# Seven half-size products in place of eight for the convolution and gate projections of a hybrid decoder layer

## What is computed

```python
proj = jnp.einsum('bld,de->ble', rmsnorm(h, norm_mix), w_in)
rq, rk, rv, rg, dqkv, dz, da, db, gate_a, gate_b = jnp.split(proj, ...)
# branch A: retention, per-head RMS norm, swish gate
o_r = rms_plain(retention(q, k, v, ...)) * jax.nn.silu(rg)
# branch B: causal convolution of width 4 and Silu over 1536 channels
xpad = jnp.concatenate([s_conv, dqkv], axis=1)
conv = xpad[:, 0:L] * conv_w[0]
for j in range(1, 4):
    conv = conv + xpad[:, j:j + L] * conv_w[j]
cq, ck, cv = split(silu(conv))          # 512 channels each
g = -exp(a_log) * softplus(da + dt_bias); beta = sigmoid(db)
o_d = gated_delta(l2norm(cq), l2norm(ck), cv, g, beta)   # a triangular solve per chunk
o_d = rms_plain(o_d) * dn_norm * silu(dz)
```

## Time and profile before

| | |
|---|---|
| median of 3 timed runs | 820.1 us (819.86 to 820.67) |
| the profiled execution | 820.44 us, span of its instructions 818.6 us |
| TensorE matmuls | 798.8 us busy, 98% of the span |
| VectorE / ScalarE / GpSimd | 403.5 / 221.5 / 154.3 us busy |
| TensorE's granted clock | 0.998 of full speed on the mean |

### The profile page before, as it was taken

One profiled execution on the slowest core, in us unless ns is written; L12 is line 12 of the kernel. 1 busy time (PEld: TensorE's weight loads), 2 busy tenths in 40 slices (PEclk: granted clock), 3 DMA queues, 4 the chain that ended last, 5 costly groups with the idle time before them and its releaser, 6 DMA issues. The chain is left out here.

```text
span 818.6 us, 12786 instructions
## 1 busy us (share of the span) xinstructions
PE 798.8 (98%) x5138; PEld 500.9 (61%) x5138; DVE 403.5 (49%) x848; ACT 221.5 (27%) x483; POOL 154.3 (19%) x182
## 2 busy tenths in 40 slices
PE   9999999999999999999999999999899999999995
PEld 4446777778879887777777776455333333334443
DVE  4223555677647424664853458726342101105976
ACT  3202152595224311131001110122121111115275
POOL 0324420041054314200220043000100001004100
PEclk9999999999999999999999999999999999999999
DMA  9620354613020200523252024035899999995211
GB/s 361 228 87 22 116 181 155 170 64 111 1 104 3 104 2 13 206 94 82 102 205 78 26 103 151 34 132 210 317 395 357 426 421 423 402 394 193 75 52 64
DMA packets 21303, 136.40 MB, mean 167 GB/s; under 512 B 2492, under 2 KB 3276, under 8 KB 13948
## 3 DMA queue, kind: packets, MB, share of 16 engines
q1 hardware_dynamic: 13328, 103.08, 32.6%
q0 software_dynamic: 4720, 23.83, 8.0%
q10 hardware_dynamic: 3196, 8.66, 3.6%
HBM read 120.12 MB, written 19.64 MB: 171 GB/s over the span
## 5 line engine op out<-in xcount | busy, mean ns | idle before, releaser
L818 PE MATMUL pair<-mem 128*128 128x288 f32 x640 | 158.4, 407 | 0.0
L818 PEld LDWEIGHTS pair<-mem 128*128 128x128 f32 x640 | 120.5, 190 | 35.7 <-ACT mem L1505 1.6
L987 PE MATMUL single<-mem 128*128 128x288 f32 x448 | 110.0, 407 | 0.3
L987 PEld LDWEIGHTS single<-mem 128*128 128x128 f32 x448 | 84.7, 190 | 25.7 <-issue 1.6
L1372 PE MATMUL single<-mem 128*32 128x512 f32 x768 | 85.1, 594 | 0.9 <-DVE mem L2543 0.9
L1505 ACT ACTIVATE mem<-single 128x256 f32<-128x256 f32 (+6 forms) x104 | 41.9, 413 | 126.8 <-PE single L1233 48.5
L1505 ACT ACTIVATE mem<-pair 128x512 f32<-128x512 f32 (+5 forms) x83 | 36.6, 488 | 143.3 <-PE pair L1320 46.8
L2536 DVE SCALAR_TENSOR_TENSOR mem<-single,mem 128x256 f32<-128x256 f32 x12 | 5.8, 485 | 102.3 <-PE single L1372 91.1
L1372 PEld LDWEIGHTS single<-mem 128*32 128x32 f32 x768 | 23.6, 110 | 52.8 <-issue 51.7
L1224 PE MATMUL pair<-mem 128*128 128x512 f32 x112 | 51.0, 601 | 0.0
L1441 PE MATMUL pair<-mem 128*128 128x512 f32 x112 | 49.4, 595 | 0.3 <-DVE mem L2604 0.3
(11 more groups left out here) (435 smaller groups left out, 1126.3 us busy)
## 6 DMA issues: line engine op xcount, KB each, us to landing
mem<-in_w_gu SPq DMA_DIRECT2D x17, 2048.0 KB, 13.6
mem<-in_w_down SPq DMA_DIRECT2D x17, 1024.0 KB, 13.4
y_slots<-mem SPq DMA_DIRECT2D x9, 512.0 KB, 9.5
y_slots<-in_zeros POOLq DMA_DIRECT2D x8, 512.0 KB, 8.7
mem<-in_w_ga SPq DMA_DIRECT2D x2, 2048.0 KB, 9.1
mem<-in_w_gb SPq DMA_DIRECT2D x2, 2048.0 KB, 8.2
mem<-in_w_wo SPq DMA_DIRECT2D x2, 2048.0 KB, 8.1
mem<-in_w_pg SPq DMA_DIRECT2D x2, 2048.0 KB, 17.1
```

Of the source, the lines that this page charges most:

```text
L818: last = nc.tensor.matmul(pb[:, hf, 0:HALF], w(k), rhs[:, k, hf * HALF:(hf + 1) * HALF], start=(k == 0), stop=(k == kk - 1))
L987: last = nc.tensor.matmul(single[plan.buf[s]][:, 0:HALF], lhs[:, k, :], rhs[:, k, :], start=(k == 0 and j in (0, 1, 3, 4)), stop=(k == 3), ...
```

## The change

All twenty blocks are computed in ten groups of two blocks, group 0 to 5 for the convolution, 6 and 7 for `rg`, 8 and 9 for `dz`. A group is seven products p1, p2, p5, p6, p3, p7, p4 of four matmuls each, 128x288, that add up in PSUM banks. ScalarE empties p1, p5, p6 and p4 (step `fa`), VectorE adds p2, p3 and p7 to what was kept (step `fd`). Four products need sums of weights. They are made by the step `fS`, four additions of 128x512 for a group, all on GpSimd. The token sums (`uS`, before `wT`) are made at the start of the stage and lie where the third place of the ring was, so the ring has two places until the last chunk.

The convolution's first tap goes to ScalarE with the small copies (step `ct`), taps 2 to 4 stay on VectorE and run over 600 columns. Silu runs over four blocks at once (128x2304), three times in all. The squares for `rN` go from GpSimd to ScalarE, `rN` is copied from PSUM first and the square root becomes a step of its own (`nS`). The small DMAs of the decay rows (`g_rows`) and the norm rows (`n_rows`) move from ScalarE's queue to SyncE's, behind the weight chunks.

```diff
@@ schedule()
-    for m in range(2, NCONV):
-        s += [("cv", m), ("cvt", m), ("cvs", m - 1)] + ([("rOt",)] if m == 2 else []) + between[m]
...
+    low = lambda g: [("cvt", 2 * g)] + sums(g + 1)
+    high = lambda g: [("ct", 2 * g + 1), ("cvt", 2 * g + 1)]
+    sums = lambda g: [("fS", g, 0), ("fS", g, 1)]
+    def middle(g, p2=(), p5=(), p6=(), p3=()):
+        return ([f(g, "p2")] + list(p2) + [f(g, "p5")] + list(p5) + [f(g, "p6")] + list(p6) + [f(g, "p3")]
+                + ([("ct", 2 * g)] if g < NCG else []) + list(p3) + [f(g, "p7")])
+    s += [("uS", 0), ("uS", 1), ("ab",), ("uS", 2), ("uS", 3), f(0, "p1"), ("abT",)]
+    s += middle(0, p6=[("abF",)]) + low(0) + ...
+    s += low(1) + [f(2, "p1"), f(1, "p4")] + high(1)
+    s += middle(2, p6=[("cvs", 0)]) + [("rN",), f(2, "p4"), ("gE", 0)] + low(2)
+    s += [f(3, "p1")] + high(2) + middle(3, p6=[("nS",), ("nr", "rN")], p3=[("gE", 1), ("gE", 2)]) + low(3)
+    s += [f(4, "p1"), f(3, "p4")] + high(3) + middle(4, p6=[("cvs", 1)], p3=[("gE", 3)] + nf[0:2]) + low(4)
+    s += [f(5, "p1"), ("gs", 0), f(4, "p4"), ("gs", 1)] + high(4)
...
@@ TensorE
-                elif k0 in ("cv", "rg", "dz"):
-                    gemm_channels(s, lambda k: w[:, k, m * P:(m + 1) * P], uT, KD)
+                elif k0 in ("fa", "fd"):
+                    lhs = {"p1": w[0][0], "p2": w[0][1], "p5": wfast[0], "p6": wfast[1], "p3": wfast[2], "p7": w[1][0], "p4": w[1][1]}[name]
+                    rhs = {"p1": fast_rows(0, 0), "p2": fast_rows(1, 0), "p5": usum[0], "p6": usum[1], "p3": fast_rows(1, 1),
+                           "p7": fast_rows(0, 1), "p4": usum[2]}[name]
+                    if name in ("p5", "p6", "p3", "p7"):
+                        pe.wait_ge(sem("fsum"), 4 * g + {"p5": 1, "p6": 2, "p3": 3, "p7": 4}[name])
+                    for k in range(4):
+                        last = nc.tensor.matmul(group_bank(s), lhs[:, k, :], rhs[:, k, :], ...)
@@ ScalarE
+                elif k0 == "ct":
+                    copy(smp[:, :, 0:3], cst[:, m, :, :])
+                    copy(cnew[:, m, 0:3], cbuf[m % 4][:, 512:515])
+                    link(copy(cnew[:, m, 3:27].rearrange("p (b l) -> p b l", b=NB), smp[:, :, 8:11]))
+                    copy(acc[m % 2][:, 0:600], cbuf[m % 4][:, 0:600], conv_w[:, m, 0:1]).then_inc(sem("cnew"), 1)
@@ GpSimd
+                elif k0 == "fS" and s[1] in POOL_SUMS:
+                    if i == 0:
+                        pool.wait_ge(sem(f"ring{place(n)}"), landed(n))
+                        if g:
+                            mm_wait(pool, ("fa", g - 1, "p6"))
+                        G.tensor_tensor(wfast[0], w[1][0], w[1][1], ALU.add).then_inc(sem("fsum"), 1)
+                        pool.wait_ge(sem("fsum"), 4 * g + 1)
+                        G.tensor_tensor(wfast[1], wfast[0], w[0][0], ALU.subtract).then_inc(sem("fsum"), 1)
+                    else:
+                        if g:
+                            mm_wait(pool, ("fd", g - 1, "p3"))
+                        G.tensor_tensor(wfast[2], w[0][1], wfast[1], ALU.subtract).then_inc(sem("fsum"), 1)
+                        G.tensor_tensor(w[1][0], w[0][0], w[1][0], ALU.subtract).then_inc(sem("fsum"), 1)
```

More of the change, by code:

```diff
@@ L185, in schedule @@
-    for m in range(2, NCONV):
-        s += [("rUs", m - 3, 0), ("rUs", m - 3, 1)] if m in (3, 4) else []
-        s += [("cv", m), ("cvt", m), ("cvs", m - 1)] + ([("rOt",)] if m == 2 else []) + between[m]
[L188 to L195, removed]
+    f = lambda g, name: (("fd" if name in ("p2", "p3", "p7") else "fa"), g, name)
@@ L196, in schedule @@
+    s += [("gA", t) for t in range(NT)] + [("l1", t) for t in range(NT)]
+    s += middle(7, p3=[("sw", 7, 0)])
     for v in LEVELS:
@@ L282 @@
 FAST = {"wx", "wy", "ux", "uy"}
+GROUP = {"fa", "fd"}
+NCG = NCONV // 2
+POOL_SUMS = tuple(range(10))
+NF_ORDER = (0, 3, 1, 2)
 KORD = [4, 5, 0, 1, 6, 7, 2, 3]
@@ L303, in own_banks @@
     if s[0] == "tmq":
-        return [("pair", s[1] // 2)] if s[1] < 4 else [("single", 0)]
+        return [("half", s[1])] if s[1] < 4 else [("single", 0)]
     return [("single", 1), ("single", 2)] if s[0] == "ss" else [("single", 3)]
@@ L314, in __init__ @@
         self.order, self.mm, self.buf, self.before, self.chunk_last = {}, {}, {}, {}, {}
-        count, nmm, npair, nsingle, last, half = {}, 0, 0, 1, {}, {}
+        count, nmm, nsingle, last, held = {}, 0, 1, {}, {}
+        age = lambda b: self.mm.get(last.get(("half", b)), 0)
         for s in self.steps:
@@ L333, in __init__ @@
                 self.buf[s] = b
[L334 to L342, removed]
+                key = ("half" if k in ("ux", "uy") and s[3] == 1 else "single", b)
+                self.before[s] = [last.get(key)]
+                last[key] = s
+            if k in GROUP:
+                nmm += 1
+                self.mm[s] = nmm
+                if s[2] == "p1":
+                    a = 0 if s[1] >= 8 or age(0) < age(3) else 3
+                    held[s[1]] = {"p1": a, "p6": a, "p7": a, "p4": a, "p2": 1}
+                    held[s[1]].update({name: 1 if s[1] >= 8 else 2 for name in ("p5", "p3")})
+                self.buf[s] = held[s[1]][s[2]]
+                key = ("half", self.buf[s])
+                self.before[s] = [last.get(key)]
+                last[key] = s
             if k == "sx":
                 nmm += 1
-                self.mm[s], self.before[s] = nmm, None
+                self.mm[s], self.before[s] = nmm, []
             if k == "wo" and s[1] == 4:
@@ L353, in __init__ @@
                 self.mm[s] = nmm
[L354 to L359, removed]
+                if k in PAIR:
+                    i = 1 if k == "sUs" else min(range(2), key=lambda i: max(age(2 * i), age(2 * i + 1)))
+                    keys = [("half", 2 * i), ("half", 2 * i + 1)]
+                else:
+                    i = nsingle % 4
+                    keys = [("single", i)]
+                    nsingle += 1
+                self.buf[s] = i
+                self.before[s] = [last.get(key) for key in keys]
+                last.update({key: s for key in keys})
             if k in CHUNK_OF:
@@ L426, in slot @@
             return BLK + 512 * i
-        ring = [view(RINGO + CHUNK_W * i, CHUNK_W) for i in range(RING)]
+        ring = [view(RINGO + CHUNK_W * i, CHUNK_W) for i in range(3)]
         uT = view(UT, KD, TOK)
@@ L501, in build @@
         dzs = view(CS + 4 * TOK, H, TOK)
[L502 removed]
+        ksq = [view(slot(i), H, DK) for i in (14, 15, 23)]
         sg = view(slot(0), KD, TOK)
@@ L801, in bank_free @@
             def bank_free(s):
-                prev = plan.before[s]
-                if prev is not None and prev[0] != "warm":
-                    ev_wait(pe, prev)
+                for prev in plan.before[s]:
+                    if prev is not None and prev[0] != "warm":
+                        ev_wait(pe, prev)
             def chunk(s):
```

436 lines of the change are left out of this document (260 added, 176 removed).

## The result

The changed kernel takes **838.25 us** (median of three, 836.92 to 838.34) against 820.1: ratio 1.0211, 95% interval 1.0197 to 1.0225. It is 18 us slower. The forecast was 820.5 with a range of 806 to 828, so it was wrong, on the slow side and outside the range. The profiled execution took 836.92 us, its span is 835.1 where before had 818.6.

A forecast was written before the change was run, and what follows sets the result against it. TensorE, busy 98% of the span, was taken as the bound. Removed products (−19.8 us), steps 1 to 8 and a vanished wait (−0.9) summed to +0.1 us, giving 820.5 us, range 806 to 828.

The forecast's parts named there:

- Step 3: Decay rows, now on SyncE's queue behind a 2 MB chunk and beside the zero fill, land late: +1.5 us (0 to 6).
- Step 8: TensorE's clock falls to half at long waits, up to two products at half rate each: +2.0 us (0 to 8).
- rival C: Clock falls at each long wait and stays low, products behind at half rate: 826 us, slower; chance 0.18.
- Step 2: p5 of group 3: GpSimd's first sum stands behind the masks of gE 0: +3.9 us, +0.3 for masks meeting taps.
- Step 4: p4 of group 3 waits for VectorE, which has the reciprocal of the norm first: +1.5 us.
- Step 5: p5 of group 4 waits behind ct, gE 1 and gE 2: +6.1 us; gE 3 costs p5 of group 5 +0.7.
- Step 1: Group 0: p3 comes late behind ScalarE's Exp, Ln, Sigmoid chain and VectorE's token sums: +0.8 us (0 to 2).
- Step 6: The solve: shorter cover over its first level, level 2's products run at the pace of GpSimd's masks: +2.0 us (1 to 3).
- Step 7: Samples' state: TensorE waits for the second addition, behind four weight sums on VectorE: +2.0 us (0 to 2.7).
- Rival D: VectorE becomes the bound, its taps slowed beside GpSimd's sums; six groups lose about 1 us each: 826.5 us; chance 0.10.
- Rival B: Sums are on time and the product count decides: 800.6 us at least, up to 812, faster; chance 0.22.
- rival A: The forecast itself: the waits eat the gain, 820.5 us, range 816 to 823.5; chance 0.50.

The follow-up runs named there:

- experiment 1: Changed kernel with the load of the decay rows issued ahead of the fifth chunk instead of behind it; 828.1 us.
- experiment 2: Changed kernel with the zero fill issued after p7 of group 6 instead of group 2, rows still behind the chunk; 825.3 us.
- version 4: Changed kernel with the decay rows ahead of the fifth chunk and GpSimd's sums of groups 3, 4 and 5 ahead of the masks; 812.9 us.
- experiment 5: Version 4 with the weight sums of groups 1 to 9 on VectorE instead of GpSimd; 821.52 us.

## Why the prediction was wrong

The mechanism was right: the removed products were there (560 records), and waits ate the gain. What was mis-sized is the sum of those waits: TensorE's waits between 82.6 and 350.1 us come to 28.9 us, over the 24 that the forecast gave as its sign of being wrong on the slow side. Step by step, measured against forecast:

- **Step 3, the decay rows: +9.9 us for +1.5 (0 to 6).** This is the step that failed. It leaned to the lone transfers "because the zero fill is spread over eight issues"; the eight were issued within 3.9 us, and the 7 MB kept the DMA engines full until 148 us. ScalarE needed the rows 12.9 us after their issue (forecast 13.6); the last part landed 22.7 us after it, beyond even the 20 that the step gave for shared transfers, and the step had left that small second DMA out. Experiments 1 and 2 each take the wait away by another road, and 14.17 falls to 4.28 and 4.27.
- **Step 8, the clock: about +6.6 us for +2.0.** From the start of p5 of group 3 to that of p6 passed 162.39 - 158.41 = 3.98 us and two more products took 4.42, against 1.94 and 3.88 in a stream: 2.6 us. The same at group 4 (3.98 and 4.48): 2.6. Behind the state update (346.94 to 350.14) 3.20 instead of 2.0, and some of the next stage: 1.2 or more; the 0.2 to make 6.6 are an estimate. The step's two products at half rate for a fall were a guess; the runs show about 2.6 us behind each of the two long waits here, and a third fall that was not expected. So rival C was nearer here than the forecast; it put 8.
- **Step 2: 4.28 us (experiment 1) for 3.9 + 0.3. Step 4: 1.35 for 1.5. Step 5: 5.82 for 6.1, and 0.84 for 0.7. Step 1: 0.99 for 0.8.** Walked from the rows of the kernel before, these came out within 0.3 us each.
- **Step 6, the solve: 0.73 + 0.43 for 2.0. Step 7: 1.61 for 2.0**, and the wait of the earlier trace rows went as forecast.
- **Missing: the price of interruptions.** A product with other matmuls on both sides takes 1.94 to 2.14 us from start to start, mostly 2.04 or more, in a stream 1.94; the kernel before has 14 stretches of products between 82 and 333 us, the changed one 30. At 0.19 each (the difference of 2.13 and 1.94) that is at most 16 x 0.19 = 3.0 us. The gain from the products is 80 x 0.243 (1.94 / 8) = 19.4, net 16.4. Counted from the timelines, start to start and without waits and the 6.4 us of low clock, the products take 156.7 us before and 140.2 here, 16.5 less, so the size holds; that the interruptions are its cause was not tried by itself. The busy time that should have come to 138.6 us came to 152.0, and to 145.2 in version 4.
- **Missing: 1.7 us within the products of k and q** (L1138), waiting for VectorE, whose taps there run beside GpSimd's sums (the first two take 3.50 us instead of 1.72). Rival D's contention, at one place: in experiment 5 these two taps take 1.63 us and the wait is 0.3. As the bound of the stage it was wrong: experiment 5 makes VectorE lighter in contention and the kernel slower.

The sum by these: -19.4 + 3.0 + 14.17 + 1.35 + 5.82 + 0.84 + 0.99 + 1.7 + 1.2 + 1.6 - 0.9 + 6.6 = +17.0; with 0.6 for a copy ahead of the last product of gA, and less 1.1 because a pause of TensorE with nothing waited for ("issue"), 1.5 us before, is 0.4 here, +16.5, and the spans differ by 16.5; an agreement this close is partly luck, as several terms are known to 0.2 us only. Of the 16.4 us between this and the forecast's +0.1, step 3 has 8.4, step 8 has 4.6, the net gain of the products 3.4. Rival B, "on time", needs both the rows and GpSimd's order changed: version 4 is that case, and its 812.9 is just above the upper end of 812 given there, since 1.35, 1.06, 1.42, 1.69 and 1.62 us of waits and the interruptions stay. Two sums of the rivals were off, without weight for the outcome: with steps 1 and 6 alone rival B comes to 803.4, not 804.5, and rival A with steps 3 and 8 at nothing to 817, not 816.

On the Trainium skill's rule in "TensorE: Matmul & The Clock Gate", "What's actually happening", that idleness throttles and activity lifts: the trace agrees that a long idle stretch ends at half clock (0.50 in 152 to 158 us and up to 162). In the stages of the change all eight waits of 4 us or more, in five of the profiles, had slow products behind them, so the loss at every long wait came as that rule has it. The contention that the Trainium skill states in "SBUF — State Buffer", "Who interferes with whom", for VectorE instructions with two SBUF inputs is seen too: taps of 600 columns took 1.05 us on the mean with GpSimd's sums beside some of them and 0.84 without. No run here shows the ports themselves.

## What to carry to other kernels

Where an engine's small chain is hidden under long blocks, cutting the blocks shortens the cover: walk each fixed order again and ask which result is waited for by the bound engine, then put that one ahead of what nobody waits for yet. Before moving a small urgent transfer behind a large one, add up the bytes of every queue in that window, not only of its own; 1 MB beside 6 MB of others took 19.1 us instead of 4.5, and the small part behind it 22.3. Look too at when the other queue's transfers start: ahead of the chunk, but beside the zero fill, the rows still took 13.6 us. A stall costs its length and often the clock behind it: here 2.6 us for each of the two longest.

## What the runs showed of the hardware

A wait of 1.6 us ahead of the last state product was followed by a half clock in the changed kernel (eight records in 3.41 us) and by none in version 4 (2.21 us), with the same 1.62 us of wait. First the changed kernel, then version 4:

```profile
345.88 1.13 PE L1280 MATMUL pair<-mem 32*128 32x512 f32 x4 [1.61 <-DVE mem L2364]
346.94 3.41 PE L1091 MATMUL pair<-mem 128*128 128x288 f32 x8
```

```profile
324.50 2.21 PE L1091 MATMUL pair<-mem 128*128 128x288 f32 x8
```

A fall therefore doesn't follow from one wait's length alone; I had expected it only behind waits of about 6 us. Also unexpected: in the kernel before and in every version but the changed kernel itself, TensorE pauses for 1.5 to 2.2 us in level 4 of the solve with nothing waited for ("issue"). The windows of version 4 show the DMA engines busy around it, at 236 to 240 us, with a chunk issued at 232.95:

```profile
236.00:238.00 2.00, 1.79 (x46) 1.38 (x41) 1.93 (x6) 1.14 (x4) 1.86 (x4) 1.00 1.04 442
238.00:240.00 2.00, 0.40 (x9) 0.40 (x9) 0.44 (x1) 0.30 (x1) 0.93 (x1) 1.00 0.83 348
240.00:242.00 2.00, 2.00 (x70) 2.00 (x69) 1.25 (x4) 0.38 (x1) 0.64 (x1) 1.00 0.05 16
```

Whether the pause comes from that traffic was not tried. Traffic alone doesn't make it: in the changed kernel the same chunk, issued at 256.98, fills the DMA engines (0.94 and 0.92 in 260 to 264 us) and TensorE is busy for 3.8 of these 4 us.
